# Output projections with four resident half-length items, tile 0 first, and the norm's scale multiplied on GpSimd

## What is computed

```python
for i in range(2):                                  # first stack
    h = rms_norm(x, g) * (1 + scale) + shift        # scale, shift, gate from c @ ada_w + b
    y = (nsa_mixer, dilated_mixer)[i](h)            # each ends in (o * silu(z)) @ w_out
    x = x + gate * y
x = rms_norm(x, final_g)
for layer in range(2):                              # second stack
    mix = (_mixer_ab, _mixer_cd)[layer](x)          # each ends in o @ w_out
    x = layer_norm(ALPHA * x + mix)
    x = layer_norm(ALPHA * x + swiglu(x))
```

## Time and profile before

| | |
|---|---|
| median of 3 runs | 1128.33 us (1127.07 to 1131.18) |
| profiled execution: time, span | 1132.87 us, 1131.1 us |
| TensorE matmul busy | 1040.2 us (92%) |
| VectorE, ScalarE, GpSimd busy | 651.9 us (58%), 473.1 us (42%), 113.0 us (10%) |
| chain that ended last | PE 76%, DVE 12%, ACT 6%, DMA 3% |
| mean granted clock of TensorE | 0.97 |

### The profile page before, as it was taken

How to read it: one execution, slowest core, us unless ns; L and a number is a source line. 1 busy time by engine, 2 the same in 40 slices (tenths; PEclk the granted TensorE clock), 3 DMA queues, 4 the chain that set the end, 5 groups by cost and what they waited for, 6 DMA issues and landing times.

```text
span 1131.1 us, 16670 instructions
## 1 busy us (share of the span) xinstructions
PE 1040.2 (92%) x6508; PEld 879.4 (78%) x6508; DVE 651.9 (58%) x1141; ACT 473.1 (42%) x698; POOL 113.0 (10%) x106
## 2 busy tenths in 40 slices
PE   5999898798998989979989999998998989999995
PEld 2799665688997777967868888886996778888884
DVE  4354453575552467635666666757334576667666
ACT  1342543333445523356334444442437533444440
POOL 2006001200880000000010000000001000000000
PEclk9999898799999889999989999999999999999998
DMA  9943344243453426520464554542542054545540
GB/s 380 365 161 131 145 166 162 84 147 115 166 176 104 149 81 235 174 79 2 149 205 167 186 203 170 204 160 90 183 160 75 1 206 158 212 167 203 187 167 37
DMA packets 23383, 178.43 MB, mean 158 GB/s; under 512 B 3711, under 2 KB 4143, under 8 KB 6823
## 3 DMA queue, kind: packets, MB, share of 16 engines
q1 hardware_dynamic: 19120, 166.70, 40.5%
q0 software_dynamic: 2224, 8.94, 2.5%
q10 hardware_dynamic: 1991, 2.14, 0.6%
HBM read 176.72 MB, written 1.05 MB: 157 GB/s over the span
## 4 chain that ended last, share of the span: by engine, by line
PE 76%; DVE 12%; ACT 6%; DMA 3%; issue 1%; POOL 1%; DVEq 0%; SPq 0%; ACTq 0%; POOLq 0%
PE G L826 13%; PE G L828 12%; PE G L827 12%; PE S L901 7%; PE T L901 7%; PE S L900 3%; PE T L900 3%; PE T L412 2%; DVE wlo L1449 2%; PE T L491 2%; PE G L507 2%; PE G L506 2%; PE G L505 1%; PE S L849 1%; ACT whi L1203 1%
## 5 line engine op out<-in xcount | busy, mean ns | idle before, releaser
L826 PE MATMUL G<-whi,hTh 128*128 128x256 f32 (+4 forms) x884 | 266.4, 301 | 16.8 <-DVE hTl L429 12.6
L827 PE MATMUL G<-wlo,hTh 128*128 128x256 f32 (+4 forms) x884 | 263.3, 298 | 0.0
L828 PE MATMUL G<-whi,hTl 128*128 128x256 f32 (+4 forms) x884 | 263.2, 298 | 0.0
L1449 DVE TENSOR_TENSOR wlo<-ring,whi 128x2048 fp32r<-128x2048 f32 (+4 forms) x56 | 152.3, 2720 | 118.1 <-ACT whi L1203 117.8
L1529 DVE TENSOR_TENSOR wlo<-ring,whi 128x2048 fp32r<-128x2048 f32 x88 | 154.4, 1758 | 92.2 <-ACT whi L1279 64.0
L826 PEld LDWEIGHTS G<-whi,hTh 128*128 128x128 f32 x884 | 168.1, 190 | 32.1 <-DVE hTl L429 24.2
L828 PEld LDWEIGHTS G<-whi,hTl 128*128 128x128 f32 x884 | 168.2, 190 | 0.3
L827 PEld LDWEIGHTS G<-wlo,hTh 128*128 128x128 f32 x884 | 168.2, 190 | 0.3
L1203 ACT CAST whi<-ring 128x2048 fp32r<-128x2048 f32 (+4 forms) x56 | 118.7, 2120 | 59.4 <-PE G L828 42.7
L901 PE MATMUL S<-hT,whi 128*128 128x512 f32 x352 | 130.2, 403 | 3.3 <-DVE hT L429 3.3
L901 PE MATMUL T<-hT,whi 128*128 128x512 f32 x352 | 126.7, 395 | 0.0
(11 more groups left out here) (261 smaller groups left out, 1591.1 us busy)
## 6 DMA issues: line engine op xcount, KB each, us to landing
ring<-in_ffn SPq DMA_DIRECT2D x44, 1536.0 KB, 6.5
ring<-in_ada_w SPq DMA_DIRECT2D x16, 1024.0 KB, 5.1
ring<-in_dil_w_in SPq DMA_DIRECT2D x16, 1024.0 KB, 4.8
ring<-in_cd_w_in SPq DMA_DIRECT2D x10, 1232.0 KB, 5.3
ring<-in_nsa_w_in SPq DMA_DIRECT2D x8, 1432.0 KB, 7.3
early<-in_ada_w SPq DMA_DIRECT2D x8, 1024.0 KB, 17.1
ring<-in_ab_w_in SPq DMA_DIRECT2D x4, 1440.0 KB, 6.5
vec<-in_vecs POOLq DMA_DIRECT2D x11, 512.0 KB, 6.5
```

What stands on the lines that cost most here:

```text
L826: pe.matmul(out_, act_h, w_h, start=first_, stop=False)
L827: pe.matmul(out_, act_h, w_l, start=False, stop=False)
L828: return pe.matmul(out_, act_l, w_h, start=False, stop=last_)
L1449: TT(wlo[k % 2][:, 0:cols], raw, whi[k % 2][:, 0:cols].bitcast(F32), ALU.subtract).then_inc(lo_done, 1)
```

## The change

**Items.** The projection's weights are four items of 512 rows by 512 columns: items 0 and 1 are the left half of the columns (first 512 rows, then the last 512), items 2 and 3 the right half. All four stay resident: item 0 in `whi0`/`wlo0`, item 1 in their last third with its low part in `out_lo1` (over `rotk`), item 2 in `whi1`/`wlo1`, item 3 in `out_hi3`/`out_lo3` (over `u`). The banks are G0 and G1 for the left half of tiles 0 and 1, G3 and G2 for the right.

**Turns.** The groups of `tok` are turned by halves: heads 0 to 7 of both tiles into the free score banks S0 and S1, inside the last rounds of the attention ("nsa", "ab", "cd") or right behind it ("dil", where six operations are reordered so that heads 0 to 7 are ready first); then heads 8 to 15 into T0 and T1.

**TensorE's order.** Item 0 over both tiles, then items 1, 2, 3 over tile 0, item 1 and 2 over tile 1, the turn of tile 0 of the norm's result, item 3 over tile 1. The four evictions are of 512 columns.

**Norm.** In the first stack GpSimd adds three of the four residual parts and multiplies by the scale.

**Next gemm.** Chunks 0 and 1 both go over tile 0, tile 1 is turned in the middle of chunk 1, then both chunks go over tile 1.

**Rest.** Item 1's cast and low part move into the attention (ScalarE behind round 2, VectorE behind round 3 in "ab" and "cd"; rounds 15 and the end in "nsa"; 7 and 8 in "dil"). The attention output is always in G2. The wait for `tab_loaded` moves from chunk 1 of `nsa_in` to behind the compression. The dummies change: one ahead of a projection (four more in "dil"), five ahead of the turn of tile 1 for the feed-forward block, one in each gemm.

The diff, cut to what matters (planning of buffers, fetches and the copies of the same edit for other engines are left out):

```diff
-OUT_C, OUT_W = 4, 256
+OUT_C, OUT_W, OUT_K = 4, 512, KT // 2
...
-            return 2 if name in ("nsa", "dil") else 2 + p % 2
+            return 2
...
@@ gpsimd
-            rstd_of(1)
+            def residual(i, scale):
+                for n, (t, half) in enumerate(((0, 0), (0, 1), (1, 0), (1, 1))):
+                    cols = slice(half * OUT_W, (half + 1) * OUT_W)
+                    part = x[:, t, cols]
+                    if n < 3:
+                        pool.wait_ge(outp["taken"], 4 * i + n + 1)
+                        tl.done(pool.tensor_tensor(part, part, tmp[:, n % 2, :], ALU.add), outp["added"])
+                    else:
+                        pool.wait_ge(outp["last"], i + 1)
+                    if scale is not None:
+                        pool.tensor_tensor(tok[:, t, cols], part, scale[:, cols], ALU.mult).then_inc(norm["scaled"], 1)
+                    if half == 1:
+                        rstd_tile(i + 1, t)
@@ tensor
+                pe.wait_ge(*turned_tile(turn_name, 0))
+                pe.wait_ge(lo_done, part0[name] + 1)
+                chunk_part(0, 0, range(KT)).then_inc(st["full"], 1)
+                pe.wait_ge(lo_done, part0[name] + 2)
+                chunk_part(1, 0, range(KT // 2))
+                turn_pe(pe, turn_name, ready, 1)
+                chunk_part(1, 0, range(KT // 2, KT)).then_inc(st["full"], 1)
+                keep_busy(1)
+                pe.wait_ge(*turned_tile(turn_name, 1))
+                for j in range(2):
+                    chunk_part(j, 1, range(KT)).then_inc(used, 1)
...
+                if not early:
+                    turn_half(i, 0, *half_ready)
+                keep_busy(1, G[3])
+                item(0, 0, 1).then_inc(used, 1)
+                pe.wait_ge(*all_ready)
+                turn_pe(pe, f"o{i}", only=2)
+                item(0, 1, 2).then_inc(used, 1)
+                turn_pe(pe, f"o{i}", only=3)
+                item(1, 0, 3).then_inc(outp["full"], 1)
+                item(2, 0, 3)
+                item(3, 0, 3).then_inc(outp["full"], 1)
+                item(1, 1, 4).then_inc(outp["full"], 1)
+                pe.matmul(S[0][:, 0:P], ident, ident, start=True, stop=True).then_inc(used, 1)
+                item(2, 1, 4).then_inc(used, 1)
+                turn_pe(pe, next_turn, next_ready, 0)
+                item(3, 1, 4).then_inc(outp["full"], 1)
...
-                if m == 1:
-                    pe.wait_ge(tab_loaded, 16)
...
-            project_out(1, "dil_out")
+            keep_busy(4, G[3])
+            project_out(1, "dil_out", (out_ready, 3), (out_ready, 4), "x0", norm_tiles(2), early=False)
...
-            att_pe(pe, "ab")
-            project_out(2, "ab_out")
-            for t in range(NT):
-                keep_busy(3 + t)
-                turn_pe(pe, "f0", norm_tiles(5), t)
+            att_pe(pe, "ab", lambda p: turn_half(2, 0, att["outs"], pairs0 + 4) if p == 8 else None)
+            project_out(2, "ab_out", None, (att["outs"], pairs0 + 8), "f0", norm_tiles(5))
+            keep_busy(5)
+            turn_pe(pe, "f0", norm_tiles(5), 1)
@@ scalar
-                turn_act(sc_e, f"o{i}")
                 sc_e.wait_ge(att["scores"], att_base[att_last] + len(att_jobs[att_last]))
-                high(name, 0, 1, KT * OUT_W)
-                high(name, 1, 0, KT * OUT_W)
-                high(name, 1, 1, KT * OUT_W)
+                high_out(name, 2)
+                turn_act(sc_e, f"o{i}", only=2)
+                turn_act(sc_e, f"o{i}", only=3)
+                high_out(name, 3)
@@ vector
+                for item in range(low_first, 2):
+                    low_out(name, item)
+                turn_low(dve, f"o{i}", only=2)
+                low_out(name, 2)
+                turn_low(dve, f"o{i}", only=3)
+                low_out(name, 3)
+                evict(0, 0, 0)
+                evict(1, 0, 1)
+                finish(0)
+                evict(2, 1, 0)
+                between()
+                turn_low(dve, turn_name, 0)
+                evict(3, 1, 1)
+                finish(1)
...
+            low("cd_in", 0, 1, KT * CD_W)
             turn_low(dve, "x1", 1)
-            low("cd_in", 0, 1, KT * CD_W)
```

More of the change, by code:

```diff
@@ L1203, in high, with high_out @@
                 sc_e.copy(whi[(k0 + j) % 2][:, 0:cols], raw).then_inc(hi_done, 1)
+            def high_out(name, item):
+                n = first[name] + item
+                sc_e.wait_ge(landed[n % 2], 16 * (n // 2 + 1))
+                if item == 0:
+                    sc_e.wait_ge(used, split0[name] - 1)
+                raw, parts = ring[:, n % 2, 0:OUT_K * OUT_W], out_high(item)
+                if item == 1:
+                    for half, part in enumerate(parts):
+                        at = half * OUT_K * OUT_W // 2
+                        ins = sc_e.copy(part, raw[:, at:at + OUT_K * OUT_W // 2])
+                else:
+                    ins = sc_e.copy((whi[0], None, whi[1], out_hi3)[item][:, 0:OUT_K * OUT_W], raw)
+                ins.then_inc(hi_done, 1)
             def take_chunk(name, st, q, j, w, silu=False):
@@ L1476, in ada_norm @@
             def ada_norm(i, mod, t):
[L1478 removed]
+                dve.wait_ge(norm["scaled"], 2 * t + 2)
                 dve.wait_ge(norm["rstd"], 2 * i + t + 1)
```

318 lines of the change are left out of this document (201 added, 117 removed).

## The result

The changed kernel takes 1120.2 us in the median of 20 runs, the kernel before 1127.4 in as many beside it: ratio 0.9931 with a 95% interval of 0.9906 to 0.9956, 0.7% faster. All ratios leave out single executions more than 1.5% above the fastest of their kernel. Forecast were 1110 and 18.7 us of gain. The time lies inside the range of 1101 to 1122, the gain is less than half of what was forecast.

What follows compares the result with a forecast made beforehand. TensorE was busy 92%, partly with dummies; the change targets waits and dummies at the attention ends. Terms -9.6 - 3.2 - 9.6 + 3.7 = -18.7 us took 1132.87 to 1114.2, scaled to 1110; range 1101 to 1122.

Steps and rivals of the forecast that it cites:

- 47.3 us to chunk 2 of `dil_in`: First mixer: chunk 2 of `dil_in` starts 47.3 us behind the first projection product, where before it was 47.9.
- second mixer: Second attention through `ab_in`'s chunk 2: -3.2 us, with the clock falling again; -6 without that fall.
- that rival: GpSimd shut out by VectorE's low parts: +7.7 us in one stage, +15.4 in both, 1117 to 1125; chance 0.08.
- Item 3: First projection: TensorE waits 2.2 us for item 3, behind item 1's low, fetch, cast and low.
- the price of the clock: Third attention and `cd_in`: half clock left out of the sums, only in the bounds (-1 per mixer, +8 in `cd_in`).
- +0.9 and +3.7: Net loss ahead of the third mixer's first product, +0.9 us, and loss in `cd_in` through waits for low parts, +3.7 us.
- My own sign: Stated sign of being wrong: half-clock windows lying over 24 us of products in the changed profile.
- half clock in the third and fourth attention, about 1120: Rival: item 1's low opens gaps of about 2 us, half clock follows, about 5 us each; chance 0.20.
- The 4.1 us of the first mixer: End of the first attention: with the earlier cast the clock does not fall, saving half of 8.2 us of busy TensorE.
- the last rival: Slower, about 1137: one half-clock stretch in each of four projections' dense products, 27.2 us in all; chance 0.06.
- Third and fourth projection up to the feed-forward: First projection product to feed-forward, third and fourth mixer: 38.6 us becomes 32.9, -5.7 each.

Runs made afterwards that it cites:

- x_after: The changed kernel, unchanged, profiled a second time; ratio to the kernel before 0.9956, profiled execution 1123.48 us.
- e3_fill: Changed kernel plus dummy matmuls in three gaps (third and fourth attention, `cd_in`); 1113.3 us, ratio 0.9878 to the kernel before.
- e2_split: Changed kernel with item 1's low part in the third and fourth attention done in halves behind rounds 3 and 4; 1109.6 us, ratio 0.9827 to the kernel before.
- b_gap: Kernel before plus two unused VectorE maxima behind round 3 of the third attention; ratio 1.0060 to the kernel before.
- e9_cdold: Changed kernel with the order of the kernel before in `cd_in` alone; ratio 0.9877 to the kernel before.
- b_fill: Kernel before plus dummies ahead of round 15's transposes in the first attention and round 8's in the second; ratio 0.9989 to the kernel before.
- b_nsa: Kernel before with the change's VectorE order in the first attention and item 0's cast a round earlier on ScalarE; ratio 0.9997 to the kernel before.
- e10_order: Changed kernel with item 1's low part halved, `cd_in`'s low part ahead of the eviction, residual additions on VectorE, no added dummies; 1102.8 us, ratio 0.9763.
- after: The first profiled execution of the changed kernel, against the kernel before; 1119.28 us.
- e1_cdlow: Changed kernel with the low part of `cd_in`'s chunk 1 ahead of the last tile's eviction and norm on VectorE; ratio 0.9896 to the kernel before.
- e6_dve: Changed kernel with the first stack's three residual additions back on VectorE; ratio 0.9910 to the kernel before.
- e7_cast14: Changed kernel with item 0's cast in the first attention back behind round 14; ratio 0.9948 to the kernel before.

## Why the prediction was wrong

**What held.** The forecast waits were met nearly one by one: 1.06 and 1.19 for 1 and 1.2 in the first attention, 5.33 for 5.6 in `cd_in`, 47.7 for 47.3 us to chunk 2 of `dil_in`, first product to feed-forward 561.70 - 528.63 = 33.1 (34.1 in x_after) for 32.9, second mixer -3.8 for -3.2 in the two pairs. `tab_loaded` brought nothing. GpSimd's additions were not shut out, and that rival falls. Item 3 was waited for 1.65 us, where 2.2 were forecast.

**The step that failed** is the price of the clock. The third attention and `cd_in` got +0.9 and +3.7 by their waits alone, with the half clock only as a bound of the range. It came: +4.5 and +6.4. The experiments settle this: the same delay with the gap filled or cut in two has a full clock and 44 to 45 us (e3_fill, e2_split), the gap in the kernel before has the half clock and 52.6 (b_gap), the old order in `cd_in` gives 7.2 us back (e9_cdold). My own sign, half clock over more than 24 us of products, came too: between 200 and 1100 us it lay over 26 and 33 us of projection and feed-forward products in the two profiles of the changed kernel, over 6 and 8 in those of the kernel before. The rival "half clock in the third and fourth attention, about 1120", to which I gave 0.20, is what happened in the third; in the fourth, with a gap of 1.78, the clock stayed in both profiles. That its number, 1120, is the measured one is partly luck: what the fourth attention did not lose, `cd_in` and `uq` did.

**A term with the wrong cause.** The 4.1 us of the first mixer: the clock did stay up there, as I had said, and the gain was even larger (10.5 for 9.0), but it is not shown to come from the clock. Taking away half of the stretch in the kernel before gave 0.6 us (b_fill), and the schedule gave 3 to 4 with a half clock still there (b_nsa). I had not read the wait of 3.00 us for VectorE ahead of the last products with V, which hid what a faster clock would have given; with it TensorE is busy at most 7.5 of the 10.5 us up to 219.29, not 8.2. That the sum for this mixer came out near is so in part luck. I had said of dummies in the last rival that half clock over them costs little, and not applied it here.

**Terms mis-sized.** Third and fourth projection up to the feed-forward brought 4.4 and 4.3 for 5.7 by the table, since a stretch at half clock at the start of the feed-forward lies in some executions of either kernel. `uq` and `ukv` stood at nothing and cost +1.5. Of my last rival, half clock in the dense products, little was seen over items 0 to 3 (2 us at the start of the third projection in x_after); it came at the start of `dil_in`, around the wait of 2.97, where the stage lost nothing by it: 129.0 us for 129.3.

**Left open.** In the second attention a gap of 1.65 to 1.70 us was followed by a half clock in twelve profiles, but in e2_split and e10_order, with the same gap and the same code, by none, nor in b_fill within 7 us. In `cd_in` the gap of 2.20 of the old order had 3.4 us of half clock about it in three of seven profiles. Nothing here tells which gap of that size will do it. The +1.5 us in `uq` comes with a half clock of 3.4 us over its first products (the stage's 36 matmuls of 384 columns take 7.8 us instead of 6.2), in every profile of the changed kernel and its variants and in none of the kernel before's. The waits ahead of it, 1.36 and 1.49 us, are the same in both kernels, so a gap alone doesn't explain it; its cause is open.

## What to carry over

A wait of TensorE can have two prices: its own length, and the half clock that may follow over busy work (here 10 us and more behind 2.3 us of idling in the third attention). So when work is moved under another engine's slack, move it in pieces, as e2_split did with gaps of 1.2 us instead of 2.3, or fill the wait with dummies (e3_fill). Before counting a recovered clock as a gain, look whether TensorE was busy in that window and what it would wait for next (b_fill).

## What the runs showed of the hardware

In the third attention, a gap of 2.3 to 2.65 us ahead of round 5's transposes was followed by a half clock of 10 us or more in each of the seven profiles that had it (after, x_after, e1_cdlow, e6_dve, e7_cast14, e9_cdold, b_gap), one of at most 1.2 us in none of the other eleven (two of them have 3.4 us near the attention's end, three ahead of its first transposes). Where TensorE is fully busy, 10.2 us at 0.53 cost about 4 us (49.0 against 45.1 with the gap filled, e3_fill), 13.6 at 0.51 about 6 (b_gap). The mean granted clock of a run of the kernel before and its time go together with a correlation of 0.93: most of what looks like noise between executions, 1121.7 to 1142.3 us in these 104 runs for the same program, goes with how long an execution was at half clock.

Not every VectorE operation that reads two SBUF operands holds GpSimd up, so the rule that the prediction took for every operation is too wide: in the kernel before, rstd on GpSimd took 0.55 us beside `x<-x,mv,vec` of 1.31 us (at 776.16), as it does alone, but 1.54 us beside `tok<-x,bias` (at 252.48); beside a low part it took 2.66 and 3.43 us in the changed kernel.
